# One GpSimd subtraction per weight unit, cut into four

## What is computed

```python
# first block, even layer: Fourier mixing and differential attention over 256 + 1024 keys
proj = h @ w_in                              # 1024 x 3072
y = jnp.concatenate([fo, ao], axis=-1) * jax.nn.silu(proj[..., G0:])
x = x + gate * (y @ w_out)
# first block, odd layer: short convolution
bg, cg, xt, g = jnp.split(h @ odd_w_in, 4, axis=-1)
x = x + gate * ((bg * conv(cg * xt) * jax.nn.silu(g)) @ odd_w_out)
# second block: a gated linear recurrence (rg), a chunked linear attention (hg), an MLP
proj = h @ w_in_2                            # 1024 x 8192
y = jax.nn.sigmoid(m_a) * y_a + jax.nn.sigmoid(m_b) * y_b
x = x + y @ w_out_2
x = x + jnp.square(jax.nn.relu(h @ w_up)) @ w_down
```

## Time and profile before

| | us |
|---|---|
| median of 3 runs | 2712.28 |
| lowest and highest | 2712.03 and 2718.73 |
| the profiled execution | 2711.57 |
| its span | 2709.6 |
| PE busy | 2653.9 (98%) |
| PE weight loads busy | 2190.4 (81%) |
| DVE busy | 1616.2 (60%) |
| ACT busy | 1014.6 (37%) |
| POOL busy | 1008.6 (37%) |

### The profile page before, as it was taken

One profiled execution on the slowest core, in us unless ns is written; L12 is line 12 of the kernel. 1 busy time (PEld: TensorE's weight loads), 2 busy tenths in 40 slices (PEclk: granted clock), 3 DMA queues, 4 the chain that ended last, 5 costly groups with the idle time before them and its releaser, 6 DMA issues.

```text
span 2709.6 us, 39203 instructions
## 1 busy us (share of the span) xinstructions
PE 2653.9 (98%) x16062; PEld 2190.4 (81%) x16062; DVE 1616.2 (60%) x1851; ACT 1014.6 (37%) x1392; POOL 1008.6 (37%) x612
## 2 busy tenths in 40 slices
PE   8999999999999999999999999999999999999997
PEld 5888878887788888788888888888787888888885
DVE  6497669866843455544556667666748433344446
ACT  4342247753433333544442322332334222222222
POOL 0254243113788843222221111111144654444552
PEclk9999999999999999999999999999999999999999
DMA  7211710034212132111121111111032111121112
GB/s 247 72 32 40 261 51 1 1 102 142 63 53 63 47 117 86 47 47 51 44 59 40 40 39 34 40 40 40 27 99 63 55 47 47 47 63 55 55 32 101
DMA packets 248541, 175.26 MB, mean 65 GB/s; under 512 B 6064, under 2 KB 236848, under 8 KB 247216
## 3 DMA queue, kind: packets, MB, share of 16 engines
q1 hardware_dynamic: 246928, 170.22, 20.4%
q10 hardware_dynamic: 1440, 2.59, 0.3%
HBM read 164.40 MB, written 8.39 MB: 64 GB/s over the span
## 4 chain that ended last, share of the span: by engine, by line
PE 70%; issue 13%; DVE 8%; POOL 4%; ACT 2%; DVEq 2%; SPq 1%; DMA 0%; POOLq 0%; ACTq 0%
PE PS L2625 11%; PE PS L2627 11%; PE PS L2626 10%; PE PS L2225 10%; PE PS L2227 10%; PE PS L2226 10%; POOL Wlo L629 3%; DVE qR L1715 2%; ACT exp L1070 1%; DVE acol L1763 1%; PE PS L2729 1%; PE PS L2736 1%; PE PS L2814 1%; PE PS L2538 1%; DVE qz L1719 1%
## 5 line engine op out<-in xcount | busy, mean ns | idle before, releaser
L629 POOL TENSOR_TENSOR Wlo<-Wraw,Whi 128x1024 fp32r<-128x1024 f32 (+1 forms) x140 | 339.5, 2425 | 984.8 <-ACT Whi L844 968.4
L2225 PE MATMUL PS<-Bh,Whi 128*128 128x512 f32 x1184 | 472.4, 399 | 5.1 <-POOL Wlo L640 1.7
L2227 PE MATMUL PS<-Bh,Wlo 128*128 128x512 f32 x1184 | 461.7, 390 | 0.0
L2226 PE MATMUL PS<-Bl,Whi 128*128 128x512 f32 x1184 | 461.0, 389 | 0.0
L2225 PE MATMUL PS<-Hh,Whi 128*128 128x512 f32 x672 | 266.0, 396 | 3.8 <-POOL Wlo L629 1.2
L2225 PEld LDWEIGHTS PS<-Bh,Whi 128*128 128x128 f32 x1184 | 222.2, 188 | 57.9 <-DVE Bl L1505 6.1
L2227 PE MATMUL PS<-Hh,Wlo 128*128 128x512 f32 x672 | 261.8, 390 | 0.0
L2227 PEld LDWEIGHTS PS<-Bh,Wlo 128*128 128x128 f32 x1184 | 222.2, 188 | 47.6
L2226 PEld LDWEIGHTS PS<-Bl,Whi 128*128 128x128 f32 x1184 | 222.4, 188 | 44.2 <-issue 0.7
L2226 PE MATMUL PS<-Hl,Whi 128*128 128x512 f32 x608 | 236.8, 390 | 0.0
L844 ACT ACTIVATE Whi<-Wraw 128x1024 fp32r<-128x1024 f32 (+1 forms) x140 | 144.5, 1032 | 162.4 <-PE PS L2227 157.6
(11 more groups left out here) (459 smaller groups left out, 5863.8 us busy)
## 6 DMA issues: line engine op xcount, KB each, us to landing
Wraw<-in_w_in SPq DMA_DIRECT2D x64, 512.0 KB, 4.0
adarow<-in_ada_rows SPq DMA_DIRECT2D x32, 512.0 KB, 6.5
Wraw<-in_odd_w_in SPq DMA_DIRECT2D x32, 512.0 KB, 4.8
Wraw<-in_w_up SPq DMA_DIRECT2D x32, 512.0 KB, 4.0
Wraw<-in_w_down SPq DMA_DIRECT2D x28, 512.0 KB, 4.2
Wraw<-in_even_w_in SPq DMA_DIRECT2D x24, 512.0 KB, 3.9
adaW<-in_ada_in SPq DMA_DIRECT2D x8, 1024.0 KB, 11.4
Wraw<-in_even_w_out SPq DMA_DIRECT2D x14, 512.0 KB, 3.6
```

Of the source, the lines that this page charges most:

```text
L629: pool.tensor_tensor(Wlo[:, slot, 0:tiles, :], Wraw[:, slot, 0:tiles, :], Whi[:, slot, 0:tiles, :].bitcast(F32), ALU.subtract).then_inc(lo ...
L2225: mm(out, Whi[:, u % 2, k, :], hi[:, k, c], start=(k == 0), stop=False)
L2226: mm(out, Whi[:, u % 2, k, :], lo[:, k, c], start=False, stop=False)
L2227: return mm(out, Wlo[:, u % 2, k, :], hi[:, k, c], start=False, stop=(k == KT - 1))
```

## The change

`split` on GpSimd issues an instruction for every two tiles in place of one for the whole unit. The wait ahead stays one wait, and `lo_ready` is raised by the last of them. `splits` and all other callers are as they were.

```diff
         def split(u, slot, tiles=KT):
 
             pool.wait_ge(hi_ready, u + 1)
-            pool.tensor_tensor(Wlo[:, slot, 0:tiles, :], Wraw[:, slot, 0:tiles, :],
-                               Whi[:, slot, 0:tiles, :].bitcast(F32), ALU.subtract).then_inc(lo_ready, 1)
+            for k in range(0, tiles, 2):
+                ins = pool.tensor_tensor(Wlo[:, slot, k:k + 2, :], Wraw[:, slot, k:k + 2, :],
+                                         Whi[:, slot, k:k + 2, :].bitcast(F32), ALU.subtract)
+            ins.then_inc(lo_ready, 1)
```

## The result

The changed kernel takes 2718.76 us (median of 18 runs, 2716.57 to 2725.21), the kernel before 2713.20 us (18 runs beside them). The ratio is 1.0023 with a 95% interval of 1.0016 to 1.0029: 4 to 8 us slower, by the medians 5.6 us. That is under the 0.3% at which the forecast draws its line, so it came out as "same", in the upper half of the range; but it is a real loss, and it lies where the forecast had looked only in part.

The account below looks back on a forecast made before the run. TensorE, busy 98% of the span, bounds the kernel; 0.78 (k units) + 1.95 (rg units) + 0.6 (convolution's opening) = 3.3 us on 2711.57, plus 0.7 for the median, gives 2715.6 us, range 2710.5 to 2721.

Parts of the forecast that it names:

- The piece and the toll: GpSimd's split at line 629: a two-tile piece takes 0.730 us, four take 2.80 against 2.40, so 0.39 us more a unit.
- k units: At 190 to 240 us, TensorE starts right after GpSimd's split; two added delays reach unit 13, 0.78 us.
- rg + 6: Unit and its three repeats, 1085 to 1400 us: TensorE already waits for the split, each adds 0.39 us.
- a piece took over 0.9 us: Sign against the forecast, at line 629, where 544 instructions near 0.73 us were expected.
- The half units: Last projections, up to 39 splits: 1.42 us are free, so 0.39 us more is hidden and TensorE doesn't wait.
- The full units have twice the matmuls beside the same split.: Units of twice the half units' 24 matmuls: the added split time was taken to be hidden there too.
- The fifth being unit rg + 2.: Unit behind the norm's opening, counted as the fifth exposed wait from 1085 to 1400 us: 0.39 of 1.95 us.
- the opening of the convolution: At 685 us VectorE gets in at three seams, 0.68 us each, so TensorE starts its unit 2.0 us later.
- That opening's net: Convolution's opening: 2.0 us later, less 1.4 given back at TensorE's wait at 716.65, leaves 0.6 us; bounds -1.4 and +2.0.
- Rival (a), the relief: VectorE near 168 us is done 1.4 us sooner, repaying the added time: 2709.5 to 2711.9; 0.23 jointly with nothing exposed.
- Rival (b), too little room: Half units' 39 splits outgrow their 1.42 us through VectorE at each seam or dearer pieces: slower, e.g. 2731; chance 0.05.
- rival (c): Interleaving at the openings alone: convolution's 2.0 us stay, early q units lose a VectorE turn, 2717 to 2720; chance 0.08.

## Why the prediction was right, and where it was not

- *The piece and the toll.* Right: 0.740 for 0.730 us, an undisturbed split 2.82 for 2.80, and the exposed tolls 0.8 us in the k units and 1.65 at rg + 6 for 0.78 and 1.56. But that is the undisturbed piece. The forecast called itself wrong if a piece took over 0.9 us; the median doesn't, the mean of 0.932 us does, and GpSimd's 150 us for 60 are the same miss: beside VectorE's work the pieces are slow in many places, at most of which nobody waits.
- *The half units.* Right that they hide it: no wait of TensorE there. The 44 pieces of 11 splits take 33.30 us, 3.03 a split, where 12 splits took 28.81, 2.40 a split; so the toll is 0.6 us here and not 0.39, well inside the 1.42:

```profile
594.00:660.00 66.00, 33.30 (x44) 1.00 0.30 89
```

- *"The full units have twice the matmuls beside the same split."* This is the step that failed. Unit 17, in the phase `g`, is a full unit, but its split starts only 1.3 us plus its own length ahead of TensorE, since ScalarE makes its high part late. I had measured the room in one stretch and argued it for the others. The row of 293.77 (2.79 us for VectorE beside the split) stood in the trace of before and said what the pieces would let in. It cost 2.1 us.
- *"The fifth being unit rg + 2."* The term was mis-sized: 0.39 us forecast, 1.8 measured, and 1.6 more for TensorE at half clock after the wait. I took it for a place of rg + 6's kind; but VectorE's first tap, 2.08 us in the trace of before, overlapped its split. Where I did look for turns, at the opening of the convolution, the forecast held: a wait of 2.35 us for 0.60 before, 1.75 us later for 2.0, and the later wait gave it back.
- *That opening's net.* +0.6 forecast, -0.7 by the traces: VectorE, held less, opens the stage 0.5 us sooner, and 1.9 us and not 1.4 return at 716 us.
- *Rival (a), the relief.* Its mechanism is there: the scaling near 168 falls from 2.84 to 1.59 us. So is the reason against it: the next one takes 3.62 instead of 2.67 us and gives most of it back. None of it reaches TensorE there; a relief that does, 0.6 us, is near 75 us, a place that the forecast didn't look at.
- *Rival (b), too little room.* Rightly left out for the half units; but its mechanism, a VectorE instruction let in at each seam, is what happened, at two units that I hadn't named. The rule of the Trainium skill that I put beside rival (a) (SBUF — State Buffer, Who interferes with whom), a lock held for a whole instruction, speaks for both sides: from it follows that whoever is cut into pieces lets the other in at each seam. The traces agree (5.85 against 2.82 us for the same four pieces with and without VectorE).
- *The sum.* 3.3 us forecast, 5.6 by the medians, 6.9 between the two traces. The tolls, the opening and the relief give 0.8 + 1.65 - 0.7 - 0.6 = 1.15 us; units 17 and rg + 2, where VectorE got in, 3.9. That is 5.05 us. The rest of the 6.9 is half clock, +1.6 and +1.8 against -1.5, of which only the 1.6 stand behind a wait that the change made.
- *The verdict.* "Same" and the range came true, but 2718.76 us is outside the 2713.5 to 2717 that had 0.62, and where rival (c) stood with 0.08. It isn't rival (c) either, for the convolution's 2.0 us were given back. That the range held is in part luck: it had been widened for other reasons than the two units that filled it.

## What to carry to other kernels

Cutting an instruction whose result is awaited as a whole buys its waiter nothing: that one gets it later by the fixed cost of each piece (0.13 us of 2.4 here) and, at every seam, by one instruction of an engine that takes turns with it, if that has one waiting. The other engine is let in sooner, which here repaid 0.6 us at one place. Cut only where somebody starts on the first piece. And before you call a cost hidden, read the room of every group of instances, not of the tightest-looking loop: the sign to look for is an instruction of the other engine that is long in the trace of before.

## What the runs showed of the hardware that I had not expected

- A VectorE tensor_scalar with one tensor input in SBUF and fp32 throughout also takes turns with GpSimd: 2.08 us beside a whole split, 1.11 us between pieces, 0.81 us when it is held back until the split is done. I had counted on instructions with two such inputs alone.
- TensorE's clock fell to 1.2 GHz for a part of a stretch after waits of 2.0 to 2.6 us, each time at a cost of some 1.5 us, but not after each such wait: behind the wait that ends at 1097.81 in the changed kernel and not behind the same wait, ended at 1099.60, with three places cut; and near 390 us in nine traces of eleven. What decides it stays open here. It is as large as the effects that this case is about, so the profiles of single executions differ by it.
- In a two-slot pipeline a shortage of room is paid once for two units, not for each: 0.53 us too little cost 8.8 us over 32 units.
